# Dealing experts to two buffers: 32 activations on ScalarE become 32 one-column scans on VectorE

## The chip, the cores and the metric

The kernel runs on one core of one Trainium2 chip. The metric is the device time of one execution in microseconds (us). The kernel before took 1589.18 us in the median of 3 runs (1584.53 to 1592.27).

The engines are TensorE (PE in the profile, PEld for its weight loads), VectorE (DVE), ScalarE (ACT), GpSimd (POOL) and SyncE (SP). Each has its own instruction stream. They wait for one another through semaphores, and SP issues nearly all bulk transfers.

## The reference

One layer of a latent-diffusion backbone on 512 latent tokens and 256 context tokens, D = 1024, all in float32. After the token mixer (a bidirectional gated recurrence) comes a mixture of experts. Its routing is what the change touches:

```python
logits = h @ router_w + router_b                 # 512 tokens x 32 experts
top_v, top_i = lax.top_k(logits, 4)
top_w = jax.nn.softmax(top_v, axis=-1)
# every expert takes its tokens in blocks, and for each block:
z = h[tok] @ w1[e] + b1[e]                       # 1024 x 2048 weights
act = clamp(z_glu) * sigmoid(1.702 * z_glu) * (clamp(z_lin) + 1)
y = (act @ w2[e] + b2[e]) * weight               # 1024 x 1024 weights
out = rmsnorm(h_lat + g2 * sum over the 4 chosen experts)
```

The reference also pads and sorts the assignments; only the sum above has to come out.

## The kernel before

Up to about 500 us the kernel computes the mixer, then the router's logits. From there on it routes, and from 518 us to about 1542 us it runs the experts.

**Blocks and steps.** A block is up to 32 (token, choice) pairs of one expert. The expert loop runs in steps of one block. Steps alternate between two parities, and each parity has its own weights in SBUF: parity 0 in `arena`, parity 1 in `big_b`. One expert's weights are 8 chunks of w1 and 4 of w2, 1 MB each. For every block GpSimd gathers the token rows from `frows` (L621), VectorE transposes them (`transpose_x`, L1248), TensorE multiplies by w1 (`z_chunk`, L1838, the last two chunks and the bias in `rest_of_z`), ScalarE and VectorE apply the gate (`gated`, L1418 to L1421), TensorE multiplies by w2 (`second`, L1870), VectorE weights the result (L1434) and GpSimd scatters it to `yrows` (L627). TensorE computes w1 of the next block before w2 of the present one (`next_z`). SP loads the next expert's chunk when a chunk is done with (semaphores `w1_used`, `w2_used`).

**The order of the first blocks.** Step 0 is expert 0 on parity 0 and step 1 is expert 1 on parity 1, whatever the routing says. Those two can start before the whole table of steps is known. From step 2 on, which expert a step takes comes from the table.

**Dealing.** The experts in a fixed order are given one after the other to the parity that has fewer blocks so far. Row n of the 32 x 33 tile holds the count n_j. The kernel before keeps `lead`, the difference of the parities: lead[j+1] = |lead[j] - n_j|. These are 32 ScalarE activations (L878), each of one column and each waiting for the one before it. They begin when VectorE has written the negated counts `n_neg` (L1339) and end with `dealt_ok`. VectorE meanwhile makes the routing weights. After `dealt_ok` it turns `lead` into the positions of the experts (L1384 to L1395, which ends with `row_ok` 5). TensorE multiplies these into the table (L1897, L1898), and VectorE writes the table's words out for the other engines (L1401 to L1409, `tab_ok`).

**The weights and what waits for them.** `kw16` holds the routing weights in three bf16 parts. VectorE computes it at L1351 to L1363 and then raises `kw_ok`. TensorE waits for `kw_ok` in the middle of the first block's w1 product, after chunk 3 of 8 (`TABLE_BEHIND`), since the matmuls at L1891 read it. It waits for `row_ok` 5 before L1897. It waits for `xt_ok` 2, the second transposed block, at the start of `next_z(0, 0)`.

**What SP waits for.** Before its loop, SP waits for `late_free`, `ring_free` and `tab_ok` in this order, and each but the last is followed by one load.

In VectorE's code, `me.mark(x)` counts x on a semaphore, `me.wait()` waits until all marked ones are done, and `me.link(x)` is both.

Of the kernel before, what the change touches and what calls it, by code (L numbers as in the profile page):

```python
# [10 lines left out]
ALU = mybir.AluOpType  # L11
ACT = mybir.ActivationFunctionType
# [51 lines left out]
def build(nc, x, c, ctx_in, c_ctx, mod_c, mod_w, mod_b, norm1_g, norm2_g, hg_w_in, hg_lb_logits, hg_norm_g,  # L64
# [7 lines left out]
    with ExitStack() as stack:  # L72
# [123 lines left out]
        so_far, lead, n_neg, behind = (rtake(E + 1)[0:E] for _ in range(4))  # L196
# [100 lines left out]
        e_v_ok e_w_ok msk_ok tab_ps row_ok dealt_ok tab_ok kw_ok late_free  # L297
# [227 lines left out]
        def _(pool):  # L525
# [69 lines left out]
            for t in (so_far, lead, behind):  # L595
                me.mark(pool.memset(t[:, 0:1], 0.0))
# [65 lines left out]
        def _(act):  # L662
# [231 lines left out]
            me.base, me.count = base + per_head * H + LT + E, 0  # L894
# [14 lines left out]
        def _(dve):  # L909
# [395 lines left out]
            for i in range(LT):  # L1305
# [33 lines left out]
            V.tensor_scalar(n_neg[:, 0:E], ps[6][0:E, 96:96 + E], -1.0, None, ALU.mult).then_inc(S["row_ok"], 1)  # L1339
            me.mark(V.tensor_tensor_scan(so_far[:, 1:E + 1], ones[0:E, 0:E], ps[6][0:E, 96:96 + E], 0.0, ALU.mult,  # L1340
                                         ALU.add))
# [3 lines left out]
            dve.wait_ge(S["e_w_ok"], LT)  # L1345
            me.mark(V.tensor_tensor(wd, wexp, msk, ALU.mult))
# [4 lines left out]
            me.link(V.tensor_reduce(es, wd, AX_X, ALU.add))  # L1351
            me.mark(V.reciprocal(es, es))
            me.mark(V.tensor_scalar(ohd[:, :, 0, :], oh[:, :, 0, :], kf[:, 0:1], None, ALU.mult))
            me.wait()
            me.mark(V.tensor_tensor(wd, wd, es.unsqueeze(2).broadcast_to([P, LT, E]), ALU.mult))
            for k in range(1, TOPK):
                to = kw16[:, :, 0, 0:E] if k == TOPK - 1 else ohd[:, :, k, :]
                me.link(V.scalar_tensor_tensor(to, oh[:, :, k, :], kf[:, k:k + 1], ohd[:, :, k - 1, :], ALU.mult, ALU.add))
            dve.sem_inc(S["late_free"], 1)
            for part in range(1, 4):  # L1360
                me.link(V.tensor_copy(kw16[:, :, part, 0:E], wd))
                if part < 3:
                    me.link(V.tensor_tensor(wd, wd, kw16[:, :, part, 0:E], ALU.subtract))  # L1363
            dve.sem_inc(S["kw_ok"], 1)
            for par in range(2):
# [601 lines left out]
```

## Time and profile before

| | |
|---|---|
| median of 3 runs | 1589.18 us |
| the profiled execution | 1585.78 us |
| its span, first to last instruction | 1584.0 us |
| TensorE busy | 1461.9 us (92%) |
| VectorE busy | 735.8 us (46%) |
| ScalarE busy | 261.3 us (16%) |
| GpSimd busy | 210.6 us (13%) |
| HBM read | 484.92 MB |
| mean granted TensorE clock | 0.961 of full |

The profiled execution is one run with the trace on. Its time is its span and 1.78 us around it. A share of busy time is a mean over stages with different limits, so it doesn't say what an edit at 520 us is worth. That is read from the stretch itself: which engine waits there, and for what.

### The profile page before, as it was taken

The numbers are of one execution on the slowest core, as the hardware profiler recorded it, in microseconds if no ns is written. First come the engines' busy times: TensorE is split into PE (matmuls) and PEld (weight loads), VectorE is DVE, ScalarE is ACT, GpSimd is POOL, SyncE is SP. The second block draws the span as 40 slices with busy tenths as digits, with TensorE's granted clock in tenths as the row PEclk, the third lists the DMA queues.
The fourth block names the chain that finished last, engine by engine and source line by source line (L and its number), as shares of the span: only waits on it lengthen the run. The fifth ranks groups of instructions, "written<-read, shape, count | busy, mean of one in ns | idle before, by whom it ended". The sixth has DMA issues, their size and how long they took to land.

```text
span 1584.0 us, 39651 instructions
## 1 busy us (share of the span) xinstructions
PE 1461.9 (92%) x14639; PEld 738.5 (47%) x14639; DVE 735.8 (46%) x2464; ACT 261.3 (16%) x467; POOL 210.6 (13%) x267
## 2 busy tenths in 40 slices
PE   5999999999896899999979999979899979999896
PEld 3658888888653333433323434323333424333232
DVE  4503877777638544443424434424343423434244
ACT  4402555555413200000000000000000000000001
POOL 1000000000051112111211111211121111212110
PEclk9999999999998999999989999979999979999798
DMA  9685211112577999998798999999799998998997
GB/s 388 192 265 148 62 54 53 53 53 57 172 306 274 358 413 407 412 415 347 301 415 339 408 417 417 414 414 417 321 417 416 417 414 321 410 417 344 413 400 295
DMA packets 130857, 497.19 MB, mean 314 GB/s; under 512 B 15356, under 2 KB 48476, under 8 KB 94892
## 3 DMA queue, kind: packets, MB, share of 16 engines
q1 hardware_dynamic: 122396, 479.93, 77.1%
q0 software_dynamic: 8256, 16.81, 2.8%
q8 instruction: 19, 0.31, 0.1%
q14 instruction: 10, 0.08, 0.0%
q10 hardware_dynamic: 176, 0.06, 0.0%
HBM read 484.92 MB, written 17.58 MB: 317 GB/s over the span
## 4 chain that ended last, share of the span: by engine, by line
PE 71%; DMA 15%; SPq 7%; DVE 4%; issue 1%; ACT 1%; ACTq 0%; DVEq 0%; POOLq 0%
PE ps L1838 28%; PE ps L1870 14%; DMA big_b<-in_moe_w 7%; PE ps L1541 6%; PE ps L1542 6%; PE ps L1543 6%; DMA arena<-in_moe_w 5%; SPq L431 4%; PE ps L1720 3%; SPq L425 2%; PE ps L1652 1%; PE ps L1564 1%; DMA arena<-in_final_g 1%; PE ps L1851 1%; PE ps L1666 1%
## 5 line engine op out<-in xcount | busy, mean ns | idle before, releaser
L1838 PE MATMUL ps<-arena,rows 128*32 128x512 f32 x2736 | 318.2, 602 | 26.7 <-DMA arena<-in_moe_w 20.1
L1838 PE MATMUL ps<-big_b,rows 128*32 128x512 f32 x2688 | 316.8, 607 | 21.8 <-DMA big_b<-in_moe_w 21.8
L886 ACT ACTIVATE rows<-ps 128x256 f32<-128x256 f32 x84 | 32.3, 385 | 977.0 <-issue 661.5
L1838 PEld LDWEIGHTS ps<-arena,rows 128*32 128x32 f32 x2736 | 86.8, 111 | 214.0 <-issue 159.2
L1838 PEld LDWEIGHTS ps<-big_b,rows 128*32 128x32 f32 x2688 | 85.5, 111 | 208.1 <-issue 153.3
L1870 PE MATMUL ps<-big_b,rows 128*32 128x256 f32 x2688 | 163.9, 395 | 8.1 <-DMA big_b<-in_moe_w 8.1
L1870 PE MATMUL ps<-arena,rows 128*32 128x256 f32 x2688 | 161.7, 392 | 9.3 <-DMA arena<-in_moe_w 8.5
L1434 DVE SCALAR_TENSOR_TENSOR y_sb<-ps,w_s,g_q 128x256 f32<-128x256 f32 x42 | 20.3, 484 | 261.0 <-PE ps L1870 261.0
L1434 DVE SCALAR_TENSOR_TENSOR rows<-ps,w_s,g_q 128x256 f32<-128x256 f32 x42 | 20.3, 484 | 256.8 <-PE ps L1870 256.8
L1870 PEld LDWEIGHTS ps<-big_b,rows 128*32 128x32 f32 x2688 | 84.2, 113 | 68.1 <-DMA big_b<-in_moe_w 12.9
L1870 PEld LDWEIGHTS ps<-arena,rows 128*32 128x32 f32 x2688 | 84.1, 112 | 67.0 <-DMA arena<-in_moe_w 13.0
L621 POOL DMA_INDIRECT rows<-frows,tok_n x86 | 88.6, 1030 | 113.8 <-issue 61.1
L1541 PE MATMUL ps<-aT_hi,wh_hi 128*128 128x512 f32 x256 | 101.8, 398 | 0.0
L1543 PE MATMUL ps<-aT_hi,wh_lo 128*128 128x512 f32 x256 | 99.8, 390 | 0.0
L1542 PE MATMUL ps<-aT_lo,wh_hi 128*128 128x512 f32 x256 | 99.8, 390 | 0.0
L627 POOL DMA_INDIRECT yrows<-y_sb,row_s x43 | 44.2, 1027 | 386.6 <-issue 386.6
L627 POOL DMA_INDIRECT yrows<-rows,row_s x43 | 44.1, 1026 | 383.9 <-issue 383.0
L1287 DVE TENSOR_SCALAR pt<-slot_io,dm_all 128x128 bf16<-128x128 f32 x340 | 74.3, 281 | 33.0 <-issue 33.0
L561 POOL TENSOR_SCALAR xv_t<-xv_t 96x1024 f32<-96x1024 f32 x1 | 2.8, 2788 | 429.1 <-DMA xv_t<-in_moe_b 429.1
L1543 PEld LDWEIGHTS ps<-aT_hi,wh_lo 128*128 128x128 f32 x256 | 48.0, 188 | 10.4
L1541 PEld LDWEIGHTS ps<-aT_hi,wh_hi 128*128 128x128 f32 x256 | 48.1, 188 | 9.9
L993 DVE TENSOR_TENSOR wh_lo<-ring_t,wh_hi 128x1024 fp32r<-128x1024 f32 x32 | 38.2, 1220 | 30.9 <-ACT wh_hi L733 30.8
(360 smaller groups left out, 1785.0 us busy)
## 6 DMA issues: line engine op xcount, KB each, us to landing
big_b<-in_moe_w SPq DMA_DIRECT2D x204, 1024.0 KB, 14.2
arena<-in_moe_w SPq DMA_DIRECT2D x180, 1024.0 KB, 15.4
ring_t<-in_hg_w_in SPq DMA_DIRECT2D x32, 512.0 KB, 3.9
ogT<-in_mod_w SPq DMA_DIRECT2D x16, 1024.0 KB, 5.0
arena<-yrows SPq DMA_DIRECT2D x8, 1024.0 KB, 12.6
x_sb<-in_x SPq DMA_DIRECT2D x2, 2048.0 KB, 7.9
arena<-in_hg_w_in SPq DMA_DIRECT2D x4, 1024.0 KB, 13.8
arena<-in_mod_c SPq DMA_DIRECT2D x4, 1024.0 KB, 19.7
```

The costliest lines, as they stand in the source:

```text
L431: sp.dma_start(to, moe_w2[bass.ds(e * FF + 2 * k * P, 2 * P), :].rearrange("(a p) n -> p a n", p=P)).then_inc(ld_w2[par][k], 16)
L621: pool.indirect_dma_start(out=xg[par], out_offset=None, in_=fquarters, in_offset=bass.IndirectOffsetOnAxis(ap=tok_n[par][:, :], axis=0), b ...
L627: pool.indirect_dma_start(out=yquarters, out_offset=bass.IndirectOffsetOnAxis(ap=row_s[par][:, :], axis=0), in_=y_sb[par], in_offset=None, ...
L993: V.tensor_tensor(wh_lo[s][:, :].rearrange("p (k n) -> p k n", k=DK), wh[:, s], wh_hi[s][:, :].bitcast(F32).rearrange("p (k n) -> p k n", ...
L1287: V.tensor_scalar(to[:, i, :], slot_io[:, :], dm_all[:, i, e], None, ALU.is_equal)
L1434: V.scalar_tensor_tensor(y_sb[par], ps[4 + par][:, 0:NW], w_s[par][:, :], g2_q[:, :], ALU.mult, ALU.mult).then_inc(S["y_ok"], 1)
L1541: mm(bank, th, mh, start=start, stop=False)
L1542: mm(bank, th, ml, start=False, stop=False)
L1543: return mm(bank, tl, mh, start=False, stop=stop)
L1720: last = mm(ps[YO_BANK[j]][:, :], ogT[:, k, i * P:(i + 1) * P], wo[n][:, k, :], start=(k == 0), stop=(k == DK - 1))
L1838: last = mm(bank[q * G:(q + 1) * G, :], XT[par][:, pos * G:(pos + 1) * G], w[:, :, q * NW:(q + 1) * NW], start=(pos == 0), stop=False)
L1870: last = mm(y[q * G:(q + 1) * G, 0:NW], aT2[:, (2 * m + a) * G:(2 * m + a + 1) * G], w2_slot(par, m, a)[:, q * NW:(q + 1) * NW], start=(m ...
```

## The change

- The 32 activations at L878 and `dealt_ok` go. The tile `n_neg` goes as well, with the VectorE instruction that wrote it.
- VectorE keeps `ahead`, the blocks of the fuller parity: ahead[j+1] = max(so_far[j+1] - ahead[j], ahead[j]), where `so_far` is the running sum of the counts. One `tensor_tensor_scan` over a single column does it, with the last value as its pointer operand for the start. `deal(first, last)` issues these, and each waits for everything marked before it.
- The 32 scans stand between other instructions: 3 ahead of the second block's index, 25 between the first block's transpose and `kw_ok`, 4 behind `kw_ok`.
- The product of `wexp` and `msk` moves behind the first transpose.
- The positions and the table now follow directly behind `kw_ok`. What step 0 needs besides (the transpose of the second block, the slots' weights, the moved rows) moves behind `tab_ok`.
- `row_ok` is counted to 4 instead of 5.

```diff
-            act.wait_ge(S["row_ok"], 4)
-            for j in range(E):
-                if j:
-                    me.wait()
-                me.mark(A(lead[:, j + 1:j + 2], lead[:, j:j + 1], ACT.Abs, bias=n_neg[:, j:j + 1]))
-            me.wait()
-            act.sem_inc(S["dealt_ok"], 1)
...
-            V.tensor_scalar(n_neg[:, 0:E], ps[6][0:E, 96:96 + E], -1.0, None, ALU.mult).then_inc(S["row_ok"], 1)
+            me.link(V.tensor_tensor_scan(so_far[:, 1:E + 1], ones[0:E, 0:E], ps[6][0:E, 96:96 + E], 0.0, ALU.mult, ALU.add))
+
+            def deal(first, last):
+
+                for j in range(first, last):
+                    me.wait()
+                    me.mark(V.tensor_tensor_scan(ahead[:, j + 1:j + 2], so_far[:, j + 1:j + 2], ahead[:, j:j + 1],
+                                                 ahead[:, j:j + 1], ALU.subtract, ALU.max))
...
-            dve.wait_ge(S["e_w_ok"], LT)
-            me.mark(V.tensor_tensor(wd, wexp, msk, ALU.mult))
+            deal(0, 3)
             dve.wait_ge(S["xi_ps"], 2)
             index(1, False)
             next_slots()
             transpose_x(0, 16)
-            me.link(V.tensor_reduce(es, wd, AX_X, ALU.add))
+            dve.wait_ge(S["e_w_ok"], LT)
+            me.mark(V.tensor_tensor(wd, wexp, msk, ALU.mult))
+            deal(3, 5)
+            me.wait()
+            me.mark(V.tensor_reduce(es, wd, AX_X, ALU.add))
+            deal(5, 7)
...
             dve.sem_inc(S["kw_ok"], 1)
+            deal(28, E)
+            me.wait()
+            me.mark(V.tensor_tensor(more, ahead[:, 0:E], ahead[:, 1:E + 1], ALU.not_equal))
...
             dve.sem_inc(S["tab_ok"], 1)
+            transpose_x(1, 16)
             dve.wait_ge(S["tab_ps"], 6)
             for par in range(2):
                 me.link(V.tensor_copy(idx_f[:, 6:9], ps[7][:, 128 + 8 * par:128 + 8 * par + 3]))
                 slot_weights(par)
                 me.wait()
-            transpose_x(1, 16)
             moved_rows(0, 0)
```

On VectorE, from the transpose of the first block on, the weights stood in this order before. The 128-partition rows are the weights.

```order
L1248 STREAM_TRANSPOSE rows<-rows 128x256
L1351 TENSOR_REDUCE ring_t<-ring_t 128x4
L1352 RECIPROCAL ring_t<-ring_t 128x4
L1353 TENSOR_SCALAR arena<-arena,kf 128x4x32
L1355 TENSOR_TENSOR ring_t<-ring_t 128x128
```

In the changed kernel the same place reads as follows. L1338 of the changed kernel is the one-column scan, which this listing names by its class of instruction.

```order
L1241 STREAM_TRANSPOSE rows<-rows 128x256
L1350 TENSOR_TENSOR ring_t<-ring_t 128x128
L1338 SCALAR_TENSOR_TENSOR ring_t<-ring_t 32x1 x2
L1353 TENSOR_REDUCE ring_t<-ring_t 128x4
L1338 SCALAR_TENSOR_TENSOR ring_t<-ring_t 32x1 x2
L1356 RECIPROCAL ring_t<-ring_t 128x4
L1338 SCALAR_TENSOR_TENSOR ring_t<-ring_t 32x1
L1358 TENSOR_SCALAR arena<-arena,kf 128x4x32
L1338 SCALAR_TENSOR_TENSOR ring_t<-ring_t 32x1 x2
L1361 TENSOR_TENSOR ring_t<-ring_t 128x128
```

Scans stand between the weights' instructions, and the product into `wd` stands behind the transpose. The scans go on in this way until the last part of `kw16`.

Further down on VectorE, behind the weights, this stood before. `bef` and `tab_words` belong to the table, and L1418 begins the gate of step 0.

```order
L1377 COPY idx_f<-ps 128x3
L1255 SCALAR_TENSOR_TENSOR w_n<-idx_f 128x1
L1248 STREAM_TRANSPOSE rows<-rows 128x256
L1372 COPY row_s<-row_n 128x1
L1373 COPY w_s<-w_n 128x1
L1384 SCALAR_TENSOR_TENSOR ring_t<-ring_t 32x32
```

In the changed kernel the table's last word is followed by them.

```order
L1413 CAST tab_e<-bef 1x116
L1415 CAST tab_words<-ring_t 1x116
L1241 STREAM_TRANSPOSE rows<-rows 128x256
L1420 COPY idx_f<-ps 128x3
L1248 SCALAR_TENSOR_TENSOR w_n<-idx_f 128x1
L1420 COPY idx_f<-ps 128x3
L1248 SCALAR_TENSOR_TENSOR w_n<-idx_f 128x1
L1400 COPY row_s<-row_n 128x1
L1401 COPY w_s<-w_n 128x1
L1424 SCALAR_TENSOR_TENSOR dm_all<-ps,ring_t 128x4x32
L1431 TENSOR_SCALAR rows<-ps 128x256
```

The transpose of the second block and the row moves went from ahead of the positions to behind the table's last word.

## Rows read from the trace of the kernel before

**Rows 1.** Chain of waits that ended last, in order of time: start us, us, what.

```profile
535.60 6.39 DMA rows<-frows,tok_n
542.51 5.36 PE ps L1838 x48
...
706.82 22.80 DMA big_b<-in_moe_w
```

**Rows 2.** Timeline of ScalarE: start us, us, line, out<-in, [idle before <-releaser].

```profile
513.06 10.42 ACT L878 ACTIVATE ring_t<-ring_t 32x1 f32<-32x1 f32 x32 [5.59 <-DVE ring_t L1339]
```

**Rows 3.** Timeline of VectorE, routing and the first step.

```profile
513.52 0.27 DVE L1346 TENSOR_TENSOR ring_t<-ring_t 128x128 f32<-128x128 f32 x1
...
517.58 0.45 DVE L1248 STREAM_TRANSPOSE rows<-rows 128x256 f32<-128x256 f32 x1 [2.61 <-DMA rows<-frows,tok_n]
517.95 0.24 DVE L1351 TENSOR_REDUCE ring_t<-ring_t 128x4 f32<-128x128 f32 x1
...
521.27 0.23 DVE L1361 CAST kw<-ring_t 128x128 bf16<-128x128 f32 x1
...
523.54 0.22 DVE L1255 SCALAR_TENSOR_TENSOR w_n<-idx_f 128x1 f32<-128x1 f32 x1
523.80 0.16 DVE L1377 COPY idx_f<-ps 128x3 f32<-128x3 f32 x1
523.99 0.22 DVE L1255 SCALAR_TENSOR_TENSOR w_n<-idx_f 128x1 f32<-128x1 f32 x1
524.25 0.45 DVE L1248 STREAM_TRANSPOSE rows<-rows 128x256 f32<-128x256 f32 x1
...
524.71 0.17 DVE L1384 SCALAR_TENSOR_TENSOR ring_t<-ring_t 32x32 f32<-32x32 f32 x1
...
526.48 0.33 DVE L1395 SCALAR_TENSOR_TENSOR ring_t<-ring_t 32x116 bf16<-32x116 f32 x1
...
527.39 0.28 DVE L1401 TENSOR_SCALAR bef<-ps 128x116 f32<-128x116 f32 x1 [0.45 <-PE ps L1898]
...
528.57 0.21 DVE L1409 CAST tab_words<-ring_t 1x116 int32<-1x116 f32 x1
...
529.47 0.42 DVE L1418 TENSOR_SCALAR rows<-ps 128x256 f32<-128x256 f32 x1 [0.24 <-DVE dm_all L1411]
```

**Rows 4.** VectorE's two 32-column and 768-column scans, from the view of one line.

```profile
L1387 DVE TENSOR_TENSOR_SCAN ring_t<-ring_t,none x1: 212/212/212, 525.0 to 525.0; 32x32 f32<-32x32 f32 x1
...
L1090 DVE TENSOR_TENSOR_SCAN arena<-res,arena x16: 1746/1750/1752, 156.5 to 422.9; 128x768 f32<-128x768 bf16 x16
```

**Rows 5.** One-column instructions without and with a pointer operand (ns min/median/max).

```profile
L1266 DVE SCALAR_TENSOR_TENSOR idx_f<-idx_f x86: 158/159/161, 510.3 to 1532.3; 128x1 f32<-128x1 f32 x86
...
L1255 DVE SCALAR_TENSOR_TENSOR w_n<-idx_f x86: 218/219/222, 523.5 to 1531.8; 128x1 f32<-128x1 f32 x86
```

**Rows 6.** Timeline of TensorE, first block and start of the second.

```profile
518.08 4.93 PE L1838 MATMUL ps<-arena,rows 128*32 128x512 f32 x32 [4.14 <-DVE rows L1248]
522.94 0.37 PE L1891 MATMUL ps<-kw,ring_t 128*128 128x3 bf16 x8
523.24 3.64 PE L1838 MATMUL ps<-arena,rows 128*32 128x512 f32 x32
...
527.14 0.21 PE L1898 MATMUL ps<-ring_t 32*128 32x116 bf16 x1
527.28 5.36 PE L1838 MATMUL ps<-big_b,rows 128*32 128x512 f32 x48
533.26 0.25 PE L1821 MATMUL ps<-ids,pt 128*128 128x6 bf16 x4 [0.62 <-DVE ids L1290]
```

**Rows 7.** Windows: busy time of each engine, then granted clock, DMA share, GB/s.

```profile
500.00:501.00 1.00, 0.89 (x16) 0.58 (x16) 0.85 (x2) 0.03 (x1) 0.00 (x0) 0.62 1.07 262
...
520.00:521.00 1.00, 1.00 (x11) 0.17 (x4) 0.81 (x4) 0.90 (x4) 0.00 (x0) 0.64 0.78 319
...
630.00:635.00 5.00, 5.00 (x56) 1.45 (x52) 2.79 (x10) 0.07 (x1) 1.19 (x2) 1.00 0.96 349
```

**Rows 8.** Timeline of SP's queue: the first load of the loop.

```profile
534.51 0.36 SPq L425 DMA_DIRECT2D big_b<-in_moe_w  x1
```

More of the change, by code:

```diff
@@ L195, in build @@
         io_one = rtake(E)[0:E]
-        so_far, lead, n_neg, behind = (rtake(E + 1)[0:E] for _ in range(4))
+        so_far, ahead, behind = (rtake(E + 1)[0:E] for _ in range(3))
         more = key
@@ L296, in build @@
         mod_used modq_ok bias_ok yo_ps h_ok stdev2_ok f_ok hT_ps hT_a hT_d lT_ps lT_ok lg_ps shb_ok cb_ps rw_ok
-        e_v_ok e_w_ok msk_ok tab_ps row_ok dealt_ok tab_ok kw_ok late_free
+        e_v_ok e_w_ok msk_ok tab_ps row_ok tab_ok kw_ok late_free
         frow_st frow_st1 pt_ok xi_ps idx_ok rows_ok go xt_ok z_ps sig_ok at_ok y_ok
@@ L594, in _ @@
                 me.mark(pool.memset(kb_row[:, n:n + 1], float((2 - n) * FAR)))
-            for t in (so_far, lead, behind):
+            for t in (so_far, ahead, behind):
                 me.mark(pool.memset(t[:, 0:1], 0.0))
@@ L1356, in _ @@
             for k in range(1, TOPK):
+                deal(2 * k + 8, 2 * k + 10)
+                me.wait()
                 to = kw16[:, :, 0, 0:E] if k == TOPK - 1 else ohd[:, :, k, :]
[L1358 removed]
+                me.mark(V.scalar_tensor_tensor(to, oh[:, :, k, :], kf[:, k:k + 1], ohd[:, :, k - 1, :], ALU.mult, ALU.add))
+            me.wait()
             dve.sem_inc(S["late_free"], 1)
             for part in range(1, 4):
[L1361 removed]
+                deal(4 * part + 12, 4 * part + 14)
+                me.wait()
+                me.mark(V.tensor_copy(kw16[:, :, part, 0:E], wd))
+                deal(4 * part + 14, 4 * part + 16)
                 if part < 3:
[L1363 removed]
+                    me.wait()
+                    me.mark(V.tensor_tensor(wd, wd, kw16[:, :, part, 0:E], ALU.subtract))
+            me.wait()
             dve.sem_inc(S["kw_ok"], 1)
+            deal(28, E)
+            me.wait()
+            me.mark(V.tensor_tensor(more, ahead[:, 0:E], ahead[:, 1:E + 1], ALU.not_equal))
+            me.mark(V.tensor_tensor(dealt[:, 0, :], so_far[:, 0:E], ahead[:, 0:E], ALU.subtract))
+            me.wait()
+            me.link(V.tensor_tensor_scan(behind[:, 1:E + 1], more, none[:, :], 0.0, ALU.not_equal, ALU.add))
+            me.link(V.scalar_tensor_tensor(dealt[:, 1, :], behind[:, 0:E], float(4 * E), dealt[:, 0, :], ALU.mult, ALU.add))
+            me.link(V.tensor_tensor(dealt, dealt, ident[0:E, 0:E].unsqueeze(1).broadcast_to([E, 2, E]), ALU.mult))
+            me.link(V.tensor_reduce(at_2, dealt, AX_X, ALU.add))
+            me.mark(V.tensor_scalar(stb16, at_2[:, 0:1].broadcast_to([E, P]), float(G), None, ALU.mult))
+            me.mark(V.scalar_tensor_tensor(end_c, by_rank[:, 0:1], 1.0, at_2[:, 1:2], ALU.mult, ALU.add))
+            me.link(V.tensor_scalar(past[0:E], io_c[0:E], at_2[:, 1:2], None, ALU.is_ge))
+            V.scalar_tensor_tensor(ind16, io_c[0:E], end_c, past[0:E], ALU.is_lt, ALU.mult).then_inc(S["row_ok"], 1)
+            me.mark(V.tensor_copy(tab_n[:, 0:1], ahead[0:1, E:E + 1]))
             for par in range(2):
@@ L1410, in _ @@
             dve.sem_inc(S["tab_ok"], 1)
+            transpose_x(1, 16)
+            dve.wait_ge(S["tab_ps"], 6)
+            for par in range(2):
+                me.link(V.tensor_copy(idx_f[:, 6:9], ps[7][:, 128 + 8 * par:128 + 8 * par + 3]))
+                slot_weights(par)
+                me.wait()
+            moved_rows(0, 0)
             me.link(V.scalar_tensor_tensor(dm, ranks, 1.0, msk, ALU.add, ALU.mult))
```

30 lines of the change are left out of this document (5 added, 25 removed).

## The prediction

> **What bounds the kernel now.** I read the chain of waits first, since it tells which stretch sets the end. The chain runs through the first gather of the loop, which lands at 541.99 us, then through TensorE's steps without a break up to about 703 us. There a burst of weight loads takes over for 22.8 us [rows 1]. In that stretch TensorE is never late for weights, but DMA is nearly full too: one of its few slack windows is 630 to 635 us at 349 GB/s [rows 7]. A shift at 535 us is thus carried by TensorE's chain, and the loads are released by TensorE's finished chunks, so they shift with it.
>
> Next comes the timeline of ScalarE, because the change removes work there. The 32 activations take 10.42 us from 513.06, so they end at 523.48 us [rows 2]. VectorE only turns to their result at 524.71 us [rows 3]. They are 1.2 us early; nothing waits for them.
>
> Then the timelines of VectorE and TensorE side by side. VectorE has the weights ready at 521.27 + 0.23 = 521.50 us [rows 3]. TensorE reaches the matmuls that read them at 522.94 us without a wait [rows 6], so the weights have 1.4 us of slack. VectorE's positions end at 526.81 us, and TensorE's table matmul starts at 527.14 us behind its own work. The gate of step 0 begins at 529.47 us [rows 3], and from there VectorE's chain leads to the index of step 2 and the gather issued at 535.60 us.
>
> **What the change removes.** 10.42 us of ScalarE, which cost nothing. One 32-column VectorE instruction also goes, and another link takes its place. I count both as 0.
>
> **One scan.** The trace has no one-column scan. Two scans give its fixed part: 768 columns take 1750 ns and 32 take 212 ns [rows 4], so a column costs (1750 - 212) / 736 = 2.09 ns and the fixed part is 212 - 31 x 2.09 = 147 ns. The scan also takes its start from a pointer. The same one-column instruction takes 159 ns without a pointer and 219 ns with one [rows 5], so that adds about 60 ns, and the scan is near 0.205 us. Each waits for the one before it. L1255 starts at 523.54 us, lasts 0.22, and the instruction that waits for it starts at 523.80 [rows 3], so the link adds 0.03 to 0.04. I take 0.24 us per scan. The lower end is no price for the pointer, 0.147 + 0.03 = 0.18. The upper end is 0.30: the 32-column scan's 0.212 as it stands, the pointer's 0.06 and the link's 0.03.
>
> The VectorE: DVE Perf Modes page of the Trainium skill (section The DRAIN you can't avoid) says that a semaphore after each instruction costs nothing extra. If that held down here, threading scans between the weights' instructions would be free of any price beyond their own durations, and the saving per scan would be 0.03 us, 0.9 us for all. The rows above show a start 0.04 us behind the end, so I don't take it.
>
> **Up to the weights.** Between the first transpose and `kw_ok` now stand 25 scans and the product that was at 513.52 us. The transpose still starts at 517.58 us, since it waits 2.61 us for the gather [rows 3]. The 3 scans ahead of the second index cost about 0.7 us, less the moved 0.27 and a wait of 0.18 that stood there, and they end inside that idle time. But the other 25 stand behind the transpose, so that idle time hides none of them. Every instruction in this stretch waits for the one ahead of it, so there is no cover either: 25 x 0.24 = 6.0, the product 0.27 + 0.03 = 0.3, and 0.15 for the reciprocal and its neighbours that overlapped before and no longer do. `kw_ok` comes at 521.5 + 6.45 = 528.0 us.
>
> **TensorE's first stall.** It reaches the weights' matmuls at 523.0 us as before and waits 5.0 us for them. The second half of the first block's w1 product then runs.
>
> **The clock.** TensorE's granted clock rose from 1.2 to 2.4 GHz at about 520.7 us (0.64 in the window 520 to 521), after 2.6 us of work. It had fallen at about 500.2 us (0.62 in that window), where TensorE had had little work since 496.9 us [rows 7]. After 5.0 us with none it will very probably have fallen again. The price is in the rows: 32 matmuls took 4.93 us at the restart of 518.08 and 3.64 us at 523.24 [rows 6], so 1.3 us. The page TensorE: Matmul & The Clock Gate of the Trainium skill (section Why this matters for your kernels) says that idle gaps between bursts of matmuls put the clock back. By that rule the 1.3 us is due; without it the sum is 1.3 us less.
>
> **The table.** Before, from the weights' matmul at 522.94 to the table's at 527.14 us were 4.2 us [rows 6]. Now it is 528.05 + 4.2 + 1.3 = 533.5 us. VectorE's positions are ready by then: 4 scans are 1.0 us, the positions 526.81 - 524.71 = 2.1, so 528.0 + 3.1 = 531.1 us. TensorE hides them. The table's words follow as before, 527.39 to 528.8 us after a matmul at 527.14: `tab_ok` is at 533.5 + 1.65 = 535.15 us.
>
> **What went behind the table.** `next_z(0, 0)` needs the transpose of the second block. Before it ran at 524.25 us with 3 us to spare. Now it starts at 535.2 and ends at 535.65 us, while TensorE was free at 533.7: a second stall of 2.0 us. From there 48 matmuls take 5.36 us as before, to 541.0 us. On VectorE the other row moves follow (0.9 + 0.1 us), the slots' ranks, and the gate of step 0, near 537.1 us. Before, the gate's start and the slots' matmul were 533.26 - 529.47 = 3.8 us apart, so VectorE would be ready at 540.9 us: as late as TensorE. The slots' matmul of step 2 stands at 541.0 us instead of 533.26, and that is +7.7 us. The gather behind it takes its 6.39 us again [rows 1], and TensorE's third block starts about 7.7 us later.
>
> **SP.** `ring_free`, which stands just ahead of the gate of step 0, comes behind the row moves at about 536.9 instead of 529.2 us, so `tab_ok` no longer decides. SP's first load of the loop started 5.3 us behind it, at 534.51 [rows 8]. That gives 542.1 us, +7.6. Its queue holds only one load before this. The load released by `late_free` goes out some 3 us later and isn't needed before 541 us. So the stream of weights and TensorE shift by the same amount, and neither catches the other.
>
> **The sum.** 0 (ScalarE) + 6.45 (scans and product) - 1.45 (slack of the weights) + 1.3 (clock) + 2.0 (transpose behind the table) - 0.6 (TensorE's wait for the slots, 0.62 in [rows 6], now gone) = 7.7 us. On the profiled execution: 1585.78 + 7.7 = 1593.5 us. That execution is 3.4 us below the median of the runs, so for the time measured I add to the median: 1589.18 + 7.7 = 1596.9 us, +0.48%. About 0.5%, 7.9 us, is what a measurement of this kernel can tell from no change.
>
> **The rivals.**
>
> Cheap scans. At 0.18 us each the 25 cost 4.5, and `kw_ok` is at 526.5 us. If the clock also stays up, the table's matmul is at 530.7 us (526.5 + 4.2), the second stall still adds 2.2, and the slots' matmul is at 530.7 + 7.5 = 538.2 us: +4.9 us, 1594.1. For it: the pointer's price is taken from another instruction. Against: a stall of 3.5 us with no work at all isn't shorter than the thin stretch behind 496.9 us. Even at no cost for a scan, the transpose behind the table leaves about +1.6 us.
>
> Clearly slower. At 0.30 us the scans cost 7.5, `kw_ok` is 1.5 us later, and if the clock falls a second time, in the stall ahead of `next_z`, the 48 matmuls lose another 1.3 us. That is 7.7 + 2.8 = +10.5 us, 1599.7. It is one mechanism, a chain of dependent small instructions in front of an engine that slows when it idles. It decides from 0.25 us per scan on, where the sum passes 7.9 us. The two stalls are only 5.5 us apart, which speaks for it; TensorE's work between them, at least 4.2 us, speaks against the second fall.
>
> The loop gives it back. TensorE waits in the loop for weights in bursts such as the one at 706.82 [rows 1]. If the loads were not tied to its progress, the first burst would eat the whole shift and the time would be 1589.2. Against it: SP's loads are released by TensorE chunk by chunk, and its start shifts too. The slack window of [rows 7] shows no backlog that could be drawn on.
>
> Faster. The gather shares the queues with the first loads of the loop. If SP's start moved more than the gather's, the 6.39 us could shrink by a few us. With scans of almost no cost (+1.6) this could end at -2 to -3 us, 1586.5. By the sums above SP's start moves as the gather's does.
>
> **How the numbers follow.** The forecast with its own range, +6 to +9 us, has 0.48; cheap scans (+3 to +6) 0.22; clearly slower 0.17; given back 0.08; faster 0.05. The forecast is split by the 7.9 us, and runs scatter by some 4 us, so a little under half of it counts as slower, and all of the third case. Slower is 0.21 + 0.17 + 0.02 = 0.40, faster by more than 0.5% is 0.04, and the same 0.56. The range from 1588 to 1601.5 us takes in cheap scans, the upper end and a part of the case given back.
>
> **What would show it.** In the profile after: 32 scans with a mean near 0.205 us and starts 0.24 us apart where two stand together. TensorE idle for 5 us in the middle of the first block's L1838 rows, with clock below 1.00 just behind. TensorE idle for 2 us before the big_b matmuls, released by VectorE's transpose. The first gather of the loop issued near 543.3 us, and from there the same pattern as before, shifted. The prediction is wrong if two scans that stand together start less than 0.15 us apart, if the clock stays at 1.00, or if the first burst of loads near 706 us no longer makes TensorE wait as long.

## The result and the profile after

The changed kernel takes 1596.76 us (median of 8 runs, 1593.96 to 1602.5). The kernel before took 1588.86 us in the same 8 rounds (1584.53 to 1593.72). The ratio is 1.0046, with a 95% interval of 1.0029 to 1.0062, which is +7.3 us (4.6 to 9.9). The prediction was 1596.9 us, from a sum of +7.7 us. The profiled execution took 1597.4 us, with a span of 1595.6 and a mean granted clock of 0.958 (before 0.961).

The page's first part shows what hardly changed. TensorE's busy time carries the restarts at the lower clock.

```profile
PE 1469.1 (92%) x14639; PEld 740.7 (46%) x14639; DVE 742.2 (47%) x2495; ACT 251.6 (16%) x435; POOL 211.2 (13%) x267
```

Next, the view of the line of the 32 scans: shortest, median and longest in ns, then the first and last start.

```profile
L1338 DVE TENSOR_TENSOR_SCAN ring_t<-ring_t x32: 200/206/208, 512.6 to 527.7; 32x1 f32<-32x1 f32 x32
```

VectorE's timeline, answering to [rows 3]: start us, us, line, out<-in, idle before and its releaser.

```profile
516.36 0.45 DVE L1241 STREAM_TRANSPOSE rows<-rows 128x256 f32<-128x256 f32 x1 [2.17 <-DMA rows<-frows,tok_n]
...
517.01 0.45 DVE L1338 TENSOR_TENSOR_SCAN ring_t<-ring_t 32x1 f32<-32x1 f32 x2
...
526.09 0.23 DVE L1372 CAST kw<-ring_t 128x128 bf16<-128x128 f32 x1
526.36 1.53 DVE L1338 TENSOR_TENSOR_SCAN ring_t<-ring_t 32x1 f32<-32x1 f32 x6
...
533.94 0.21 DVE L1415 CAST tab_words<-ring_t 1x116 int32<-1x116 f32 x1
534.31 0.45 DVE L1241 STREAM_TRANSPOSE rows<-rows 128x256 f32<-128x256 f32 x1 [0.16 <-DVE tab_words L1415]
...
535.54 0.15 DVE L1400 COPY row_s<-row_n 128x1 uint32<-128x1 uint32 x1
535.61 0.14 DVE L1401 COPY w_s<-w_n 128x1 f32<-128x1 f32 x1
```

A pair of scans takes 0.45 us, so two starts are 0.45 - 0.206 = 0.24 us apart. From the transpose at 516.36 to 526.85 us the chain doesn't break: each instruction starts at most 0.04 us behind the end of the one before (once 0.15), or overlaps it. The second transpose stands behind the load table, at 534.31 us.

TensorE's timeline for the same stretch, answering to [rows 6]:

```profile
516.86 5.10 PE L1851 MATMUL ps<-arena,rows 128*32 128x512 f32 x32 [3.85 <-DVE rows L1241]
526.92 0.37 PE L1904 MATMUL ps<-kw,ring_t 128*128 128x3 bf16 x8 [4.96 <-DVEq L1378]
527.22 5.04 PE L1851 MATMUL ps<-arena,rows 128*32 128x512 f32 x32
...
532.52 0.21 PE L1911 MATMUL ps<-ring_t 32*128 32x116 bf16 x1
534.81 5.36 PE L1851 MATMUL ps<-big_b,rows 128*32 128x512 f32 x48 [2.08 <-DVE rows L1241]
540.10 0.26 PE L1834 MATMUL ps<-ids,pt 128*128 128x6 bf16 x4
...
549.43 7.05 PE L1851 MATMUL ps<-arena,rows 128*32 128x512 f32 x48 [2.92 <-DVE rows L1241]
```

The reader sees three things. TensorE idles for 4.96 us in the middle of its first block, and for 2.08 us ahead of the second. The 32 matmuls behind the first idle time take 5.04 us in place of 3.64. And the third block, behind the gather, takes 7.05 us for 48 matmuls. Before, that block ran at full speed behind a wait of 2.36 us:

```profile
542.51 5.36 PE L1838 MATMUL ps<-arena,rows 128*32 128x512 f32 x48 [2.36 <-DVE rows L1248]
```

Windows of the profile after (length of the window, busy time of PE, PEld, DVE, ACT, POOL, then granted clock, DMA share, GB/s) show the clock fall at the end of the first wait and behind the gather, its lower level (0.50, which is 1.2 GHz) behind the first wait, and the return at 530 us:

```profile
526.00:527.00 1.00, 0.08 (x3) 0.08 (x4) 0.75 (x5) 0.00 (x0) 0.00 (x0) 0.84 1.01 410
528.00:529.00 1.00, 1.00 (x12) 0.27 (x8) 0.86 (x6) 0.00 (x0) 0.00 (x0) 0.50 0.18 70
530.00:531.00 1.00, 1.00 (x14) 0.24 (x8) 0.27 (x5) 0.00 (x0) 0.00 (x0) 0.96 0.00 0
550.00:551.00 1.00, 1.00 (x16) 0.24 (x11) 0.93 (x7) 0.00 (x0) 0.00 (x0) 0.78 1.05 438
```

The first gather of the loop, in the chain of waits, answers to [rows 1]. SP's queue answers to [rows 8].

```profile
542.44 6.47 DMA rows<-frows,tok_n
```

```profile
541.23 3.62 SPq L425 DMA_DIRECT2D big_b<-in_moe_w  x5
```

The first transpose runs at 517.58 us before and at 516.36 after, because its gather landed 1.22 us earlier in this execution. I therefore count from this transpose, T:

| from T, us | before | after | difference | predicted |
|---|---|---|---|---|
| weights ready | 3.92 | 10.49 | +6.57 | +6.45 |
| weights' matmuls start | 5.36 | 10.56 | +5.20 | +5.1 |
| table's matmul starts | 9.56 | 16.16 | +6.60 | +6.4 |
| second block starts | 9.70 | 18.45 | +8.75 | +8.4 |
| slots' matmul | 15.68 | 23.74 | +8.06 | +7.7 |
| SP's first load | 16.93 | 24.87 | +7.94 | +7.6 |
| third block starts | 24.93 | 33.07 | +8.14 | +7.7 |
| third block's slots' matmul | 30.22 | 40.06 | +9.84 | +7.7 |

From there the shift is carried. The start of each step's weighting on VectorE (L1434 before, L1447 after) shows it. Before:

```profile
562.58 0.48 DVE L1434 SCALAR_TENSOR_TENSOR rows<-ps,w_s,g_q 128x256 f32<-128x256 f32 x1 [4.91 <-PE ps L1870]
...
703.85 0.48 DVE L1434 SCALAR_TENSOR_TENSOR y_sb<-ps,w_s,g_q 128x256 f32<-128x256 f32 x1 [5.26 <-PE ps L1870]
...
1541.34 0.48 DVE L1434 SCALAR_TENSOR_TENSOR y_sb<-ps,w_s,g_q 128x256 f32<-128x256 f32 x1 [5.26 <-PE ps L1870]
```

After:

```profile
571.19 0.49 DVE L1447 SCALAR_TENSOR_TENSOR rows<-ps,w_s,g_q 128x256 f32<-128x256 f32 x1 [4.52 <-PE ps L1883]
...
712.46 0.48 DVE L1447 SCALAR_TENSOR_TENSOR y_sb<-ps,w_s,g_q 128x256 f32<-128x256 f32 x1 [5.22 <-PE ps L1883]
...
1551.70 0.48 DVE L1447 SCALAR_TENSOR_TENSOR y_sb<-ps,w_s,g_q 128x256 f32<-128x256 f32 x1 [5.23 <-PE ps L1883]
```

The shift is 8.61 us at 562.58, the same 8.61 at 703.85, and 10.36 us at 1541.34. In between it changes only where a burst of loads makes TensorE wait: to 11.13, 9.95, 11.56, 9.33 and 11.33, among others. These changes have both signs. The first of these bursts, behind 706 us, was one of the prediction's signs. TensorE's timeline there, before:

```profile
713.86 1.06 PE L1838 MATMUL ps<-big_b,rows 128*32 128x512 f32 x8 [1.61 <-DMA big_b<-in_moe_w]
...
715.04 3.66 PE L1870 MATMUL ps<-arena,rows 128*32 128x256 f32 x64
```

After:

```profile
722.29 1.93 PE L1851 MATMUL ps<-big_b,rows 128*32 128x512 f32 x8 [1.61 <-DMA big_b<-in_moe_w]
...
724.36 5.46 PE L1883 MATMUL ps<-arena,rows 128*32 128x256 f32 x64
```

In this burst TensorE waits 3.4 us for loads before (0.17 + 1.65 + 1.61) and 3.5 us after (1.85 + 1.61), so the burst doesn't take the shift back. What differs is the clock: in the profile after it fell in the burst (64 matmuls in 5.46 us in place of 3.66), and the shift is 9.95 us behind it.

Below, "the stretch" is the time from T to the weighting of the third block: 562.58 - 517.58 = 45.0 us before and 571.19 - 516.36 = 54.8 us after. It measures the effect at its place, free of what the bursts add later. Each kernel has one profile, so a stretch has no interval of its own.

### The profile page after: what moved, and what is told of

It is laid out like the page before. It is cut to its first block, busy times and chain, and to the rows that moved or that the text cites. A ratio compares the mean times of both kernels' runs of the same rounds, so it can differ in the third digit from the quotient of the medians.

```text
span 1595.6 us, 39649 instructions
## 1 busy us (share of the span) xinstructions
PE 1469.1 (92%) x14639; PEld 740.7 (46%) x14639; DVE 742.2 (47%) x2495; ACT 251.6 (16%) x435; POOL 211.2 (13%) x267
## 4 chain that ended last, share of the span: by engine, by line
PE 72%; DMA 15%; SPq 6%; DVE 4%; issue 1%; ACT 1%; ACTq 0%; DVEq 0%; POOLq 0%
PE ps L1851 28%; PE ps L1883 15%; DMA big_b<-in_moe_w 7%; PE ps L1554 6%; DMA arena<-in_moe_w 6%; PE ps L1555 6%; PE ps L1556 6%; SPq L431 3%; PE ps L1733 3%; SPq L425 2%; PE ps L1665 1%; PE ps L1577 1%; DMA arena<-in_final_g 1%; PE ps L1864 1%; PE ps L1679 1%
## 5 line engine op out<-in xcount | busy, mean ns | idle before, releaser
L1851 PE MATMUL ps<-arena,rows 128*32 128x512 f32 x2736 | 324.5, 612 | 24.3 <-DMA arena<-in_moe_w 17.3
L1447 DVE SCALAR_TENSOR_TENSOR y_sb<-ps,w_s,g_q 128x256 f32<-128x256 f32 x42 | 20.3, 484 | 260.9 <-PE ps L1883 260.9
L1447 DVE SCALAR_TENSOR_TENSOR rows<-ps,w_s,g_q 128x256 f32<-128x256 f32 x42 | 20.4, 485 | 251.7 <-PE ps L1883 251.7
L1556 PEld LDWEIGHTS ps<-aT_hi,wh_lo 128*128 128x128 f32 x256 | 48.1, 188 | 10.3
L1554 PEld LDWEIGHTS ps<-aT_hi,wh_hi 128*128 128x128 f32 x256 | 48.1, 188 | 9.9
```

Of the source, the lines that this page charges most:

```text
L1447: V.scalar_tensor_tensor(y_sb[par], ps[4 + par][:, 0:NW], w_s[par][:, :], g2_q[:, :], ALU.mult, ALU.mult).then_inc(S["y_ok"], 1)
L1554: mm(bank, th, mh, start=start, stop=False)
L1556: return mm(bank, tl, mh, start=False, stop=stop)
L1851: last = mm(bank[q * G:(q + 1) * G, :], XT[par][:, pos * G:(pos + 1) * G], w[:, :, q * NW:(q + 1) * NW], start=(pos == 0), stop=False)
```

## The experiments

My theory: the scans stand in VectorE's unbroken chain up to the weights and make TensorE wait; the clock falls in that wait; the transpose behind the table makes it wait again; the loop carries all of it to the end. The main rival was that the loop gives the shift back. Each kernel was timed in 5 rounds against the kernel before. A ratio's interval of +-0.0016 is +-2.5 us. The rounds of the last two variants of the changed kernel ran on another chip, where the kernel before took 1592.05 us, so times are compared only within the same rounds.

**The moves alone.** The kernel before, with the second transpose, the slot weights and step 0's row moves behind the table's words:

```diff
             dve.sem_inc(S["kw_ok"], 1)
-            dve.wait_ge(S["tab_ps"], 6)
...
-                slot_weights(par)
...
-            transpose_x(1, 16)
-            moved_rows(0, 0)
...
+            transpose_x(1, 16)
+            dve.wait_ge(S["tab_ps"], 6)
...
+                slot_weights(par)
...
+            moved_rows(0, 0)
```

> ScalarE deals as before and the scans are not there; only step 0's row moves and the second block's transpose stand behind the table. I measure the stretch from the start of VectorE's first transpose (L1248) to the start of the third block's weighting: 45.0 us before, 54.8 us after. My theory: TensorE waits 2.0 us for the second transpose ahead of the big_b matmuls and gets 0.6 us back at the slots' matmul, so the stretch is 46.5 us; the time is +1.5 us on before (ratio 1.001). Rival, the order of the row moves costs nothing and all of the loss is in the scans: 45.0 us and ratio 1.000.

Measured: ratio 1.0036 (1.0016 to 1.0056), +5.7 us; stretch 48.1 us (46.5 expected). TensorE's timeline:

```profile
529.37 5.36 PE L1837 MATMUL ps<-big_b,rows 128*32 128x512 f32 x48 [2.08 <-DVE rows L1248]
534.65 0.26 PE L1820 MATMUL ps<-ids,pt 128*128 128x6 bf16 x4
...
543.69 7.05 PE L1837 MATMUL ps<-arena,rows 128*32 128x512 f32 x48 [2.26 <-DVE rows L1248]
```

The second stall is there with the predicted size, and the slots' matmul comes 17.25 us behind T (517.40) in place of 15.68, +1.6 us. The other 1.5 us of the stretch come from the third block at 7.05 us in place of 5.36, less 0.2 us of a shorter gather. The clock fell behind a wait of 2.26 us, whereas before it held behind 2.36 us. The total is above what the stretch gives; only the lower half of its interval fits. But this profile is the fastest of the kernel's 12 executions: 1589.04 us, with a median of 1593.90. It is 3.3 us above the profiled execution of before (1585.78), and that does agree with its stretch.

**The scans alone.** The changed kernel, with the second transpose, the slot weights and the row moves ahead of the positions again (the two instructions that write `sel` too, as before):

```diff
             deal(28, E)
+            dve.wait_ge(S["tab_ps"], 6)
...
+            transpose_x(1, 16)
+            moved_rows(0, 0)
...
             dve.sem_inc(S["tab_ok"], 1)
-            transpose_x(1, 16)
-            dve.wait_ge(S["tab_ps"], 6)
...
-            moved_rows(0, 0)
```

> The 32 scans on VectorE as in the changed kernel, but the second transpose and the row moves ahead of the positions again, as before. My theory: kw_ok stays 10.5 us behind the first transpose, TensorE stalls 5.0 us for it and restarts at the low clock, but doesn't stall ahead of the big_b matmuls. The slots' matmul of step 2 comes 22.3 us behind the first transpose (15.7 before, 23.7 after). The stretch is 53.4 us, or 51.7 if the clock doesn't fall again behind the gather; ratio 1.0045. Rival, the row moves' place is worth nothing once the scans delay the table: 54.8 us.

Measured: ratio 1.0046 (1.003 to 1.0062), +7.3 us; stretch 51.5 us (51.7 expected if the clock holds).

```profile
527.91 0.38 PE L1904 MATMUL ps<-kw,ring_t 128*128 128x3 bf16 x8 [5.03 <-DVEq L1378]
528.21 4.96 PE L1851 MATMUL ps<-arena,rows 128*32 128x512 f32 x32
533.58 5.36 PE L1851 MATMUL ps<-big_b,rows 128*32 128x512 f32 x48
...
548.82 5.36 PE L1851 MATMUL ps<-arena,rows 128*32 128x512 f32 x48 [2.73 <-DVE rows L1241]
```

The first stall and its restart are there, the second stall is gone. The third block kept its clock here, behind 2.73 us. The stretches of the two parts add up: +3.1 and +6.5 are 9.6 of the 9.8 us. The fall behind the gather is in the part of the moves by one profile each; that it belongs to the moves isn't shown. Without it the two stretches are +1.4 and +6.5, and the changed kernel's +8.1. Their totals add to 13.0 against 7.3 us, each known to about 3 us. So the split is read from the stretches; the totals don't settle it.

**Does the loop give a shift back?** The 25 scans behind T are done twice, with the same values:

```diff
-                for j in range(first, last):
+                for j in [j for j in range(first, last) for _ in range(2 if 3 <= j < 28 else 1)]:
```

> The changed kernel with each of the 25 scans between the first transpose and kw_ok done twice. The value is the same. Theory that the scans are a serial chain of 0.235 us each with no cover, carried to the end: kw_ok 16.4 us behind the first transpose instead of 10.5, the stretch 60.7 us, the time 5.9 us above the changed kernel, ratio to before 1.0085. Rival, the loop of weight loads gives shifts back: the stretch is 60.7 us but the time stays within 2 us of the changed kernel, ratio 1.005.

Measured: ratio 1.011 (1.008 to 1.014), +17.5 us (12.7 to 22.3); stretch 62.6 us (60.7 expected), +17.6.

```profile
534.97 0.37 PE L1904 MATMUL ps<-kw,ring_t 128*128 128x3 bf16 x8 [11.12 <-DVEq L1378]
535.28 5.32 PE L1851 MATMUL ps<-arena,rows 128*32 128x512 f32 x32
```

The wait grows from 4.96 to 11.12 us, 6.2 for 25 scans, 0.25 each. The stretch grows by 7.8 us over the changed kernel's: besides the wait, 1.3 are a longer gather (7.79 us in place of 6.47) and 0.3 the clock (5.32 in place of 5.04). Stretch and total grow alike. The rival that the loop gives it back falls.

**Keeping the clock up, first try.** Idle matmuls whose result nobody reads, 9 ahead of the wait for the weights and 6 ahead of the block behind the gather:

```diff
+            def filler(n):
+                for _ in range(n):
+                    mm(ps[5][:, :], ident[:, :], w1_slot(0, 0)[:, 0:512], start=True, stop=True)
```

> The changed kernel with idle matmuls (results not used) in two of TensorE's stalls: 9 ahead of the wait for kw_ok, 6 ahead of the first block behind the gather. All waits stay. Theory that the clock is a term of its own: granted clock stays at 1.00 from about 520 us on, the 32 matmuls behind the weights take 3.6 instead of 5.0 us, the 48 behind the gather 5.4 instead of 7.05 us, and the stretch is 51.8 us, 3.0 less; time 3 us less than the changed kernel, ratio to before 1.003. Rival, the loss is the waits alone and the slow restart is hidden behind VectorE: 54.8 us.

Measured: ratio 1.009 (1.0061 to 1.0119); stretch 58.2 us (51.8 expected).

```profile
523.42 7.99 PE L1890 MATMUL ps<-arena,ident 128*128 128x512 f32 x18
531.54 3.64 PE L1851 MATMUL ps<-arena,rows 128*32 128x512 f32 x32
...
537.73 7.05 PE L1851 MATMUL ps<-big_b,rows 128*32 128x512 f32 x48 [2.08 <-DVE rows L1241]
```

I had mis-sized them: each took 0.89 us (two records). The first nine held the weights' matmuls until 531.25 us, 13.3 us behind T in place of 10.6, and the six behind the gather ended 0.9 us too late. What it does show: the 32 matmuls take 3.64 us when work fills the gap. And the second block took 7.05 us behind the same wait of 2.08 us behind which it took 5.36 after. Of the total it says nothing.

**Second try.** The same with 256 columns: 10 ahead of the weights, 4 ahead of the second block, 6 behind the gather.

```diff
+                    mm(ps[5][:, 0:256], ident[:, :], w1_slot(0, 0)[:, 0:256], start=True, stop=True)
```

> The changed kernel with idle matmuls in three of TensorE's stalls, half as wide as in the run warm and fewer, so that they end before the wait does: 10 ahead of kw_ok, 4 ahead of the second transpose, 6 ahead of the first block behind the gather. Theory that the clock is a term of its own: the clock stays at 1.00 from about 521 us on, the 32 matmuls behind the weights take 3.64 us, the 48 behind the gather 5.36 us, and the stretch from the first transpose to the third block's weighting is 51.7 us against 54.8 in the changed kernel; ratio to before 1.003. Rival, only the waits count: 54.8 us and ratio 1.005.

Measured: ratio 1.0035 (1.002 to 1.005), +5.6 us; stretch 52.8 us (51.7 expected).

```profile
523.41 4.58 PE L1890 MATMUL ps<-arena,ident 128*128 128x256 f32 x20
528.54 0.36 PE L1911 MATMUL ps<-kw,ring_t 128*128 128x3 bf16 x8 [0.54 <-DVEq L1378]
528.83 3.64 PE L1851 MATMUL ps<-arena,rows 128*32 128x512 f32 x32
...
550.67 5.36 PE L1851 MATMUL ps<-arena,rows 128*32 128x512 f32 x48 [1.14 <-DVE rows L1241]
```

All blocks behind the weights run at full speed. The slots' matmul stands 22.34 us behind T (517.98) in place of 23.74: the clock's part of the first shift is 1.40 us. Behind the gather it is another 1.69. The stretch gains only 2.1 of these 3.1 us, since the gather took 7.5 us in this run and 6.5 in the profile after. So the clock's part is read from the timelines; the totals, 1.0035 against 1.0046, don't tell the two kernels apart.

**Scans in VectorE's idle time.** Ten of the 25 scans stand ahead of the first transpose, where VectorE waits for the gather:

```diff
             next_slots()
+            deal(3, 13)
             transpose_x(0, 16)
...
-            deal(3, 5)
...
-                deal(2 * k + 8, 2 * k + 10)
+                deal(max(2 * k + 8, 13), max(2 * k + 10, 13))
```

> The changed kernel with 10 of its 25 scans (j = 3 to 12) ahead of VectorE's first transpose, where VectorE idles 2.2 us for the gather, instead of behind it. The other 15 stay. My theory: the transpose starts at most 0.2 us later, kw_ok comes 8.2 us behind it instead of 10.5, TensorE stalls 2.7 us for the weights instead of 5.0, and the stretch from the transpose to the third block's weighting is 52.5 us, or 51.1 if the clock survives the shorter stall; ratio to before 1.003. Rival, what costs is not the scans' length but that TensorE must stop and restart: 54.8 us.

Measured: ratio 1.0035 (1.0019 to 1.0052); stretch 53.5 us (52.5 expected).

```profile
526.86 0.36 PE L1902 MATMUL ps<-kw,ring_t 128*128 128x3 bf16 x8 [1.89 <-DVEq L1376]
```

The weights' matmuls start 8.24 us behind T (8.2 expected), so the ten scans no longer stand in front of them. They aren't quite free: they last until the transpose starts, at 518.62 us with no idle time ahead of it, so that they and no longer the gather decide T. What they add ahead of T (0.2 us expected) isn't in the stretch. The gather of the loop took 7.18 us here, 0.7 more than after. The clock fell all the same behind a wait of 1.89 us (32 matmuls 5.26 us), and again behind the gather (48 matmuls 7.05 us).

**The wait moved behind the whole block.** TensorE's wait for the weights and its 8 small matmuls stand behind `rest_of_z(0, 0)`:

```diff
-                if pos == TABLE_BEHIND:
-                    pe.wait_ge(S["kw_ok"], 1)
...
-                    last.then_inc(S["tab_ps"], 1)
             rest_of_z(0, 0)
+            pe.wait_ge(S["kw_ok"], 1)
...
+            last.then_inc(S["tab_ps"], 1)
```

> The changed kernel with TensorE's wait for kw_ok, and the 8 small matmuls behind it, moved from after chunk 3 of the first block to the end of that block, ahead of the table's matmuls. My theory: TensorE does the rest of the first block while VectorE scans, and then waits for the positions instead (row_ok comes 13.7 us behind the first transpose). The table's matmul is 13.8 us behind the transpose instead of 16.2, and the stretch from the transpose to the third block's weighting is 52.5 us against 54.8, up to 1.7 us more or less with where the clock falls; ratio to before 1.003. Rival, the bound is VectorE's chain alone and TensorE's place of waiting is worth nothing: 54.8 us, ratio 1.005.

Measured: ratio 1.0056 (1.0038 to 1.0075); stretch 55.0 us. A miss of 2.5 us (52.5 expected), with a part of its reason in TensorE's timeline:

```profile
534.93 0.62 PE L1864 MATMUL ps<-bias,sel 96*32 96x512 bf16 x4 [3.42 <-DVE sel L1394]
```

The block ends with the bias matmuls, and their operand `sel` is written behind the positions. I had moved one wait behind another that came later still. The table's matmul came 14.85 us behind T, 1.0 later than expected, and the second block took 6.73 in place of 5.36 us, at the lower clock. So `sel` is written ahead of the first transpose in the next one:

```diff
             next_slots()
+            for par in range(2):
+                V.tensor_scalar(sel[par][:, :], pmod[0:96, :].broadcast_to([96, G]), float(par), None,
+                                ALU.is_equal).then_inc(S["sel_ok"], 1)
             transpose_x(0, 16)
```

> The run late, and besides the two instructions that write sel moved from behind the positions to ahead of the first transpose. In late TensorE's bias matmuls waited 3.4 us for them. My theory: they were what took the wait's place. Now TensorE does the whole first block while VectorE scans, waits only for the positions, and the table's matmul is 13.9 us behind the first transpose (16.2 in the changed kernel). The stretch from the transpose to the third block's weighting is 52.5 us, or up to 1.7 us off with where the clock falls; ratio to before 1.003. Rival, VectorE's chain alone is the bound: 54.8 us, ratio 1.005.

Measured: ratio 1.0042 (1.0023 to 1.006); stretch 55.6 us (52.5 +- 1.7 expected).

```profile
535.85 7.45 PE L1851 MATMUL ps<-big_b,rows 128*32 128x512 f32 x48 [2.08 <-DVE rows L1241]
```

The table's matmul came 13.85 us behind T, as expected (13.9), so `sel` had cost 1.0 us. But then the clock fell ahead of the second block (7.45 in place of 5.36 us) and once more behind the gather, which itself took 7.42 us. These 2.1 us and 0.9 of the gather are the miss of 3.1. The fall ahead of the second block is the one that the prediction had put into its slower rival.

**All three together.** This one has the wait behind the block, `sel` early, ten scans in the idle time, and the second transpose ahead of the positions. The 32 scans stay on VectorE.

```diff
+            deal(3, 13)
             transpose_x(0, 16)
...
             dve.sem_inc(S["kw_ok"], 1)
             deal(28, E)
+            transpose_x(1, 16)
```

> Dealing on VectorE with all that these runs point to: late2, 10 scans in VectorE's idle time for the gather, and the second transpose ahead of the positions. The row moves stay behind the table. My theory: positions 11.8 us behind the first transpose, the table's matmul 12.1 us (9.6 before, 16.2 in the changed kernel), no second stall, and VectorE's row moves on the way to the gate: the stretch is 48.3 us, up to 1.7 more where the clock falls; ratio to before 1.002. So it stays behind the kernel before. Rival, the scans can be hidden in full: 45.0 us, ratio 1.000.

Measured: 1592.22 against 1592.05 us for the kernel before in the same rounds, ratio 1.0007 (0.9986 to 1.0027); stretch 48.0 us (48.3 expected).

```profile
530.37 0.26 PE L1907 MATMUL ps<-ring_t 32*128 32x32 bf16 x4 [2.22 <-DVE ring_t L1393]
530.62 5.36 PE L1849 MATMUL ps<-big_b,rows 128*32 128x512 f32 x48
...
537.27 0.25 PE L1832 MATMUL ps<-ids,pt 128*128 128x6 bf16 x4 [1.29 <-DVE ids L1283]
538.25 5.35 PE L1881 MATMUL ps<-arena,rows 128*32 128x256 f32 x64 [0.72 <-issue]
```

The 4.96 us in the middle of the first block and the 2.08 us ahead of the second are gone. What is left are 2.22 us ahead of the table and 1.29 ahead of the slots. The clock fell behind the last, and the 64 matmuls of w2 took 5.35 in place of 3.66 us. That isn't on the path here, since the third block still waited 0.86 us for the gather. The stretch is 3.0 us longer than before, and as in the run with ten scans moved it begins right behind them. The total can't tell this kernel from the kernel before, but its interval reaches +4.3 us, so the 3.0 us may well be there: the scans are cheaper like this, and not shown to be free.

**Is there something to gain over the kernel before?** Three kernels try it. The first adds 4 idle matmuls of 256 columns to the kernel before, ahead of its first block:

```diff
+            for _ in range(4):
+                mm(ps[5][:, 0:256], ident[:, :], w1_slot(0, 0)[:, 0:256], start=True, stop=True)
```

> The kernel before (dealing on ScalarE) with 4 idle matmuls of 256 columns where TensorE waits 4.1 us for the first transpose. Theory that the restart at the low clock at 518 us is on the path: the first 32 matmuls take about 3.7 us instead of 4.93, the stretch from the first transpose to the third block's weighting is 43.7 us instead of 45.0, ratio 0.999. Rival, VectorE's weights (kw_ok 3.9 us behind the transpose) or its positions become the bound: 45.0 us, ratio 1.000.

Measured: ratio 0.9998 (0.9987 to 1.0009); stretch 45.6 us (43.7 expected).

```profile
517.94 3.64 PE L1838 MATMUL ps<-arena,rows 128*32 128x512 f32 x32 [0.29 <-DVE rows L1248]
...
541.23 7.05 PE L1838 MATMUL ps<-arena,rows 128*32 128x512 f32 x48 [2.23 <-DVE rows L1248]
```

The first 32 matmuls gain 1.29 us, and the third block loses 1.69 again: the clock fell behind a wait of 2.23 us.

The second also takes the slots of step 2 ahead of the gate of step 0, so that the gather starts earlier:

```diff
-            gated(0, 0)
             one_hot(2, 0)
             slots_after(0, 0)
+            gated(0, 0)
...
-            next_z(0, 0)
-            slots_of(3)
+            pe.wait_ge(S["xt_ok"], 2)
+            for pos in range(AHEAD):
+                z_chunk(ps[3], 1, pos, 16)
+                if pos == AHEAD - 2:
+                    slots_of(3)
```

> The run prewarm, and besides step 2's one-hot tiles and index on VectorE ahead of step 0's gate instead of behind it, with the slots' matmul on TensorE behind 5 of the 6 chunks of the second block. My theory: the gather of step 2 is what TensorE waits for (2.4 us), and it is issued 15.2 us behind the first transpose instead of 18.0; the third block starts 22.1 us behind it instead of 24.9, and the stretch is 42.2 us; ratio 0.998. Rival, w2 of step 0 then waits for the gate and eats the gain: 43.7 us.

Measured: ratio 0.9988 (0.9975 to 1.0); stretch 43.7 us, the rival's number. The gather no longer makes TensorE wait, but the gate comes later:

```profile
533.39 5.35 PE L1870 MATMUL ps<-arena,rows 128*32 128x256 f32 x64 [2.05 <-DVE rows L1421]
```

TensorE waits 2.05 us for it, and the 64 matmuls behind take 5.35 in place of 3.66 us. So the third fills that wait with 4 more idle matmuls:

```diff
+            for _ in range(4):
+                mm(ps[5][:, 0:256], ident[:, :], w1_slot(0, 0)[:, 0:256], start=True, stop=True)
```

> The run best with 4 more idle matmuls of 256 columns where TensorE waits 2.05 us for step 0's gate ahead of its w2. In best the clock fell there and w2 of step 0 took 5.35 us instead of 3.66. Theory: the clock stays up, w2 takes 3.66 us, the stretch is 42.0 us against 43.7 in best and 45.0 before, ratio to before 0.998. Rival, the gather of step 2 then ends last and eats it: 43 us or more, ratio 0.999.

Measured: ratio 0.9992 (0.9972 to 1.0013); stretch 43.3 us (42.0 expected), and all blocks of the stretch at full speed. The rival was right here: the third block waited 1.05 us for a gather of 7.41 us. It is 1.7 us shorter in the stretch, which these runs can't tell from nothing. Nor does the gain last in the profiles: the weightings were 1.8 us ahead of the kernel before at 703.85 us and 0.3 us ahead at 730.80, behind the first burst of loads (1.7 and 0.0 in the run best). In both the clock fell in that burst, where it held before. No version beat the kernel before by more than the measurement's uncertainty.

## Why the prediction was right

**ScalarE's 32 operations** went at no gain. Nothing in the profile after starts earlier for it, as [rows 2, 3] said.

**The scans** were priced from two wider scans and the pointer's share [rows 4, 5] at 0.205 us, with 0.24 from start to start. They measured 0.206 and 0.24. By TensorE's wait, the doubled scans give 0.25 each. The term of 6.45 us measured 6.57. The rival of cheap scans fell with the scan's duration, and the slower rival's 0.30 us a scan too. The Trainium skill's page VectorE: DVE Perf Modes, section The DRAIN you can't avoid, says that a semaphore after each operation costs nothing extra, and also that a next operation that isn't held starts earlier. For these short instructions the trace agrees with the second and not with the first: the two copies at 535.54 and 535.61 us, with no wait between them, start 0.07 us apart at 0.15 us each, while linked ones start 0.03 to 0.04 us behind the end.

**The slack** of 1.4 us was used up first, as predicted. The wait was 4.96 us.

**The clock** fell in the first stall: 5.04 against 3.64 us, 1.40 where 1.3 was said. The second set of idle matmuls took just that away.

**The second transpose** behind the table cost 2.08 us where 2.0 was said. It is there without the scans and gone when only the scans stay.

**Not foreseen** was the clock's fall behind the gather, +1.69 us in the third block. The sum stopped at that block's start, with the sentence that from there the pattern is as before. In this profile it makes the stretch +9.8 in place of +7.7 us. The slower rival did have a second fall, but ahead of `next_z`, where the block took its 5.36 us. So it is in part luck that the forecast of the total came out better than its parts: the stretch says +9.8, the medians say +7.3 (4.6 to 9.9), and +9.8 lies at the interval's upper end. Some of the gap is in the profile of before, which is of a fast execution: 1585.78 us is 3.1 below the median of the 8 rounds, while the one after is 0.6 above its own.

**The gather** took 6.47 us in place of 6.39, so the faster rival had nothing to draw on. Its premise was also off: the list of DMA queues has GpSimd's transfers in q0 and the loads in q1, and they share only the 16 engines.

**The loop** carries the shift. That was argued from SP's loads, which TensorE releases, and the doubled scans show it: +17.6 in the stretch, +17.5 in the total. The first burst made TensorE wait as long as before.

What stays open: why the moves alone cost +5.7 us in total with +3.1 in the stretch. Its profile is the fastest of 12 executions, at a mean granted clock of 0.963; the slowest, 1602.75 us, had 0.954. So the clock may hold in some executions and fall in others, behind the gather and in the bursts. No run here repeats a profile of the same kernel, so where it falls in the others isn't shown.

## What to carry to other kernels

A chain of linked small instructions costs its count times the sum of duration and link wherever it stands between an input's arrival and the first result that another engine waits for; on an engine that nobody waited for, the same chain was free. Price the wait that it makes and also TensorE's restart behind it, and look at every later wait in which TensorE does little. Before something is moved behind something else, look for the next reader of it on every engine: here the second transpose cost 2.1 us by its place alone, and a wait that was moved past `sel` only changed its name.

## What the runs showed of the hardware

Whether the granted clock falls in TensorE's wait behind the gather isn't decided by how long the wait is. It held behind 2.36 us (before) and 2.73 (the scans alone), and fell behind 2.23 (idle matmuls ahead of before's first block), 2.26 (the moves alone), 2.92 (after), 3.32, 3.65, 4.19 and 4.23. Ahead of the second block the wait was 2.08 us in seven profiles; the clock held in four of them (48 matmuls in 5.36 us) and fell in three (6.73, 7.05 and 7.45 us). In the first block it fell behind 1.89 us. The fall needn't come in the wait itself: behind the gather it came 1.1 us after TensorE had resumed (after, at about 550.6 us) and 1.0 us (the moves alone, at 544.7), in windows of half a us. A fall costs a block 1.3 to 1.7 us here, and 2.1 in one run.

The first gather of the loop took 6.2 to 7.8 us in the twelve profiles whose chain of waits holds it. These 1.6 us are as large as a fall of the clock. Each is of another kernel, so how much of it is scatter isn't shown.
